# A one-core encoder step: first and last expert pair loaded in quarter matrices, last down weights by column blocks

## The reference, cut to what matters

```python
g_idx = argmax(x @ w_grp + b_grp)            # 4 groups
top_v, top_i = top_k(e_logits[g_idx], 2)     # 2 of the 4 experts in it
gate = one_hot(eid, 16) * g_w * softmax(top_v)
h = silu(einsum('nd,edf->nef', x, w1)) * einsum('nd,edf->nef', x, w3)
h = h * gate[..., None]
h_out = h_in + einsum('nef,efd->nd', h, w2)
y = rmsnorm(h_out) * g_final                 # y_prompt, y_sample
```

## Time and profile before

| | |
|---|---|
| median of 3 runs | 2102.23 us |
| the profiled execution: own time | 2103.92 us |
| its span, first to last instruction | 2102.1 us |
| busy: TensorE, VectorE, ScalarE, POOL | 96%, 29%, 12%, 3% |
| mean granted TensorE clock | 0.984 |
| chain that ended last: TensorE, DMA | 88%, 9% |
| DMA rate over the span; in the expert stage | 192 GB/s; 428 GB/s |

### The profile page before, as it was taken

How to read it: one execution, slowest core, us unless ns; L and a number is a source line. 1 busy time by engine, 2 the same in 40 slices (tenths; PEclk the granted TensorE clock), 3 DMA queues, 4 the chain that set the end, 5 groups by cost and what they waited for, 6 DMA issues and landing times.

```text
span 2102.1 us, 26593 instructions
## 1 busy us (share of the span) xinstructions
PE 2024.6 (96%) x11213; PEld 1359.1 (65%) x11213; DVE 606.6 (29%) x1622; ACT 255.3 (12%) x617; POOL 61.9 (3%) x116
## 2 busy tenths in 40 slices
PE   7999999999999999999999999999996999999996
PEld 4767788877777777777777777776773333333332
DVE  3053222212212443534535435321003222121212
ACT  2121112121201010110101101000011000000002
POOL 0010000000000000000000000000000000000000
PEclk9999999999999999999999999999997999999998
DMA  9563444433234132331332314266433999999996
GB/s 296 96 192 122 134 126 148 159 124 121 84 121 148 58 125 89 118 125 42 125 116 92 125 42 140 104 215 215 160 131 129 428 428 428 427 427 428 427 428 253
DMA packets 190666, 404.31 MB, mean 192 GB/s; under 512 B 11520, under 2 KB 165840, under 8 KB 176848
## 3 DMA queue, kind: packets, MB, share of 16 engines
q1 hardware_dynamic: 182064, 380.95, 49.7%
q0 software_dynamic: 6112, 18.61, 3.2%
q10 hardware_dynamic: 2368, 3.02, 0.4%
HBM read 391.87 MB, written 10.67 MB: 191 GB/s over the span
## 4 chain that ended last, share of the span: by engine, by line
PE 88%; DMA 9%; DVE 1%; DVEq 1%; issue 0%; ACT 0%; SPq 0%; ACTq 0%
PE bank L739 21%; PE bank L943 19%; PE bank L1155 7%; PE bank L945 6%; PE bank L1086 6%; PE bank L737 5%; PE bank L1188 3%; PE bank L1205 3%; PE bank L1053 3%; DMA ring<-in_w 3%; DMA Z<-in_w 3%; DMA SC<-in_w 3%; PE bank L988 1%; PE bank L994 1%; PE bank L716 1%; PE bank L852 1%
## 5 line engine op out<-in xcount | busy, mean ns | idle before, releaser
L739 PE MATMUL bank<-uT,ring 128*128 128x288 f32 (+2 forms) x1792 | 455.2, 411 | 0.6 <-DVE uT L1558 0.6
L943 PE MATMUL bank<-uT,ring 128*128 128x288 f32 x1536 | 406.4, 414 | 0.0
L739 PEld LDWEIGHTS bank<-uT,ring 128*128 128x128 f32 (+2 forms) x1792 | 334.2, 189 | 99.1 <-issue 8.2
L943 PEld LDWEIGHTS bank<-uT,ring 128*128 128x128 f32 x1536 | 283.1, 190 | 78.5 <-issue 3.1
L1155 PE MATMUL bank<-ring,Z 128*64 128x512 f32 x480 | 138.5, 611 | 7.0 <-issue 7.0
L945 PE MATMUL bank<-Z,ring 128*128 128x288 f32 x512 | 140.5, 418 | 0.0
L1086 PE MATMUL bank<-SC,ring 128*128 128x288 f32 x512 | 128.5, 410 | 1.1 <-DVEq L345 1.1
L1155 PE MATMUL bank<-Z 128*64 128x512 f32 x336 | 119.3, 615 | 5.1 <-issue 5.1
L737 PE MATMUL bank<-ring,Z 128*128 128x256 f32 x512 | 117.4, 383 | 0.0
L1086 PEld LDWEIGHTS bank<-SC,ring 128*128 128x128 f32 x512 | 96.1, 190 | 29.5 <-DVEq L345 1.6
L945 PEld LDWEIGHTS bank<-Z,ring 128*128 128x128 f32 x512 | 92.8, 190 | 25.5 <-issue 1.4
(11 more groups left out here) (385 smaller groups left out, 1796.2 us busy)
## 6 DMA issues: line engine op xcount, KB each, us to landing
ring<-in_w_in SPq DMA_DIRECT2D x102, 1024.0 KB, 7.9
ring<-in_w SPq DMA_DIRECT2D x42, 2048.0 KB, 31.5
Z<-in_w SPq DMA_DIRECT2D x33, 2048.0 KB, 30.5
SC<-in_w SPq DMA_DIRECT2D x21, 2048.0 KB, 29.4
ring<-in_w_mem_kv SPq DMA_DIRECT2D x16, 1024.0 KB, 6.8
ring<-in_w_o SPq DMA_DIRECT2D x16, 1024.0 KB, 7.6
ring<-in_p_b SPq DMA_DIRECT2D x8, 1024.0 KB, 5.3
ring<-in_p_m SPq DMA_DIRECT2D x8, 1024.0 KB, 8.0
```

Of the source, the lines that this page charges most:

```text
L739: ins = mm(bank[t][0:w, 0:T], rslot[q][:, c, w0:w0 + w], uT[:, c, :], start=c == 0, stop=c == KC - 1)
L943: ins = mm(b[:, 0:T], rslot[q][:, c, P * t:P * t + P], uT[:, c, :], start=c == 0, stop=c == last - 1)
```

## The change

1. In pair 0 and pair 7 a fill of w1 or w3 now holds a quarter of the rows of one matrix for both experts (the order is w1, w3 of quarter 0, w1, w3 of quarter 1 and so on). `up_fine` works in 8 steps of one fill each, and every step signals. A row piece that one DMA packet brings is 8 KB where it was 16 KB.
2. The last four fills (w2 of pair 7) hold 512 columns of both experts each, as two DMAs of 1 MiB in pieces of 2 KB. `last_down` finishes one bank with each of them and scatters the prompt tokens' block by block; the sample tokens come at the end.
3. The final norm's gain is multiplied into columns 0 to 1023 of `H` before the factor is known (`with_gain`), from two tiles that POOL loads early. ScalarE then scales these columns by the factor and sends them out from its own queue; VectorE does columns 1024 to 2047 in one piece for each tile, and `gains` loads half as much.
4. POOL's early loads grow from three to six, and TensorE and VectorE wait for all of them (`nk_in` 96).

```diff
+        K_COL = 12 * NPAIR - 4
+        def fine(i):
+            return i in (0, NPAIR - 1)
+        def hp_upto(i, fills):
+            return sum(8 if fine(x) else 4 for x in range(i)) + (fills if fine(i) else (fills + 1) // 2)
...
-        gB = ring[2][:, 0:D]
-        gB2 = ring[2][:, D:D + 512]
+        gB = (CON[:, K_M2:K_M2 + 512], Z_t[:, 15424:15936], ring[2][:, 0:1024])
+        gB2 = ring[2][:, 1024:1536]
...
+                if j_ < 8 and fine(i):
+                    q, w = divmod(j_, 2)
+                    return a[("w1", "w3")[w]][0][2 * i:2 * i + 2, 512 * q:512 * q + 512, :].rearrange("e (p c) n -> p e (c n)", c=4)
...
+                b = j_ - 8
+                return a["w2"][0][2 * i:2 * i + 2, :, 512 * b:512 * b + 512].rearrange("e (p c) n -> p e c n", c=4)
...
-                        sp.wait_ge(s("hp_mm"), 4 * i + j_ // 2 + 1)
+                        sp.wait_ge(s("hp_mm"), hp_upto(i, j_ + 1))
...
+                sp.wait_ge(s("hp_mm"), hp_upto(NPAIR - 1, 4))
                 gains()
...
+            for g in range(2):
+                pload(gB[g], dram_g[KC + 4 * g:KC + 4 * g + 4, :].rearrange("c p -> (c p)").partition_broadcast(P), "nk_in")
...
+                def up_fine(i):
+                    for st in range(8):
+                        q, w = divmod(st, 2)
+                        wv = arrived(12 * i + st).rearrange("p (x c n) -> p x c n", x=2, c=4)
+                        if w == 0:
+                            pe.wait_ge(s("xg_ev"), 4 * i + q + 1)
...
+                        for c in range(4):
+                            for x in range(2):
+                                ins = mm(bank[2 + w][sides[x], :], XG[:, 4 * q + c, sides[x]], wv[:, x, c, :],
+                                         start=q == 0 and c == 0, stop=q == 3 and c == 3)
+                        ins.then_inc(s("hp_mm"), 1)
+                        if st == 1 and i + 1 < NPAIR:
+                            pe.wait_ge(s("xg_ev"), 4 * i + 4)
+                            prepare(i + 1)
...
+                    columns(0)
+                    columns(1)
+                    pe.wait_ge(s("gp_ev"), i + 1)
+                    scatter(0)
+                    columns(2)
+                    scatter(1)
+                    columns(3)
+                    scatter(2)
+                    scatter(3)
+                    for g in range(4):
+                        ins = mm(bank[4][TS * g:TS * g + TS, :], GP[:, i % 2, TP:T], Yk[:, 512 * g:512 * g + 512], start=True, stop=True)
...
+            def left_half(tt):
+                act.wait_ge(s("rs_fin"), tt + 1)
+                A(H[:, tt, 0:1024], H[:, tt, 0:1024], ACT.Copy, scale=rsm[:, tt:tt + 1]).then_inc(s("y_left"), 1)
+                act.wait_ge(s("y_left"), tt + 1)
+                act.dma_start(o["y_p"][P * tt:P * tt + P, 0:1024], H[:, tt, 0:1024]).then_inc(s("out_y"), 16)
+            final_root(0)
+            token_squares(True, 8)
+            final_root(1)
+            left_half(0)
+            final_root(2)
+            left_half(1)
...
+                for g in range(4):
+                    for tt in range(2):
...
+                        V.tensor_tensor(h, h, bank[2 * (g % 2) + tt][:, :], ALU.add).then_inc(s("fin_add"), 1)
+                    if 1 <= g <= 2:
+                        with_gain(g - 1)
+                out_norm(0)
```

More of the change, by code:

```diff
@@ L582, in _ @@
             for t in range(2):
[L583 to L586, removed]
+                sp.wait_ge(s("y_done"), t + 1)
+                sp.dma_start(o["y_p"][P * t:P * t + P, 1024:2048], H[:, t, 1024:2048]).then_inc(s("out_y"), 16)
+            sp.wait_ge(s("y_done"), 3)
             for g in range(4):
@@ L1206, in down, with last_down, columns, scatter @@
                         ins.then_inc(s("sc_mm2"), 1)
+                def last_down(i):
+                    pe.wait_ge(s("hid_done"), i + 1)
+                    for f in range(4):
+                        ins = nc.tensor.transpose(bank[2][:, P * f:P * f + P], hid[:, f:f + 509:4], ident)
+                    ins.then_inc(s("ht_mm"), 1)
+                    pe.wait_ge(s("sc_add"), 9 * i)
+                    pe.wait_ge(s("ht_ev"), i + 1)
+                    def columns(b):
+                        wv = arrived(12 * i + 8 + b).rearrange("p (x c n) -> p x c n", x=2, c=4)
+                        for c in range(4):
+                            for x in range(2):
+                                ins = mm(bank[4 + b][sides[x], :], HS[:, c, sides[x]], wv[:, x, c, :], start=c == 0, stop=c == 3)
+                        ins.then_inc(s("yk_mm"), 1)
+                    def scatter(g):
+                        pe.wait_ge(s("yk_ev"), 4 * i + g + 1)
+                        for tt in range(2):
+                            t0, tn = TOK[tt]
+                            if g >= 2:
+                                pe.wait_ge(s("fin_add"), 2 * (g - 2) + tt + 1)
+                            mm(bank[2 * (g % 2) + tt][:, :], GP[:, i % 2, t0:t0 + tn], Yk[:, 512 * g:512 * g + 512],
+                               start=True, stop=True).then_inc(s("sc_mm2"), 1)
+                    columns(0)
[9 more added lines that the diff above has]
+                        ins = mm(bank[4][TS * g:TS * g + TS, :], GP[:, i % 2, TP:T], Yk[:, 512 * g:512 * g + 512], start=True, stop=True)
+                    ins.then_inc(s("sc_mm2"), 1)
                 prepare(0)
@@ L1212, in _ @@
                 gathered(0, range(4))
-                for i in range(EXPERTS // 2):
-                    up(i)
+                for i in range(NPAIR - 1):
+                    if fine(i):
+                        up_fine(i)
+                    else:
+                        up(i)
                     down(i)
+                up_fine(NPAIR - 1)
+                last_down(NPAIR - 1)
             with pe.Else():
@@ L2093, in _ @@
                         rows_in(i + 1)
-                    for n in range(9):
+                    for n in range(0 if last else 9):
                         tt, g = divmod(n, 4)
@@ L2144, in _ @@
                 dve.sem_inc(s("fin_add"), 9)
+                with_gain(0)
+                with_gain(1)
                 out_norm(0)
```

98 lines of the change are left out of this document (62 added, 36 removed).

## The result

The changed kernel takes 2095.78 us, the median of 8 runs (2095.35 to 2098.50), the kernel before 2102.48 in the same session (8 runs, 2101.79 to 2104.58): ratio 0.9968, 95% interval 0.9959 to 0.9976, or 6.7 us less. Forecast were 9.4 us less, 2092.8, and a range of 2089.8 to 2098.0. The profiled execution is the median one: its own time is 2095.78, its span 2094.0.

The account below looks back on a forecast made before the run. The expert-weight stream was taken to bound the kernel, with an open head and tail. Head -3.5, block 3's start +1.6 and tail -7.5 sum to -9.4 us: median 2102.23 becomes 2092.8, range 2089.8 to 2098.0.

Parts of the forecast that it names:

- What bounds the kernel: From some 1626 us the expert-weight stream bounds; a microsecond gained at its head or tail is one off the time.
- Head, -3.5: Pair 0's first step, 8 matmuls instead of 16, frees a buffer sooner: tenth fill issued 3.5 us earlier.
- The feared hole at the third fill: Rival: after pair 0's first step a late third fill leaves a hole up to 3.5 us: 2096.3; chance 0.10.
- The stream, +1.5: Last landing 1.5 us later from smaller pieces: +1.2 for four column fills at 403 GB/s, +0.3 for 8 KB pieces.
- packets cost more: Rival: column blocks run at the 1 KB rate, 354 GB/s; last landing moves by +4.4: 2095.6; chance 0.12.
- TensorE and DMA meet at block 3: In pair 7's end, block 3 lands at 2076.15 and TensorE starts it at 2076.4: a term of +1.6 us.
- Tail, -7.5: Work from block 3's start to the end takes 19.8 us instead of 27.3; bounds 18.5 to 22.
- 19.8: Tail's last step: VectorE's last product at 15.3 us plus 4.5 for stores, 2.36 MB being just inside.
- ScalarE's stores ending last: Sign at the kernel's end that, if seen, would show the prediction wrong.
- third rival: Last block lands late for another reason; only the head and norm's part (some 2 us) remain: 2098 to 2100; chance 0.04.
- Edits at nothing: POOL's three more loads, ScalarE's moved table load and the halved gains behind the last fill cost nothing.
- Slower by TensorE's clock: Rival: short waits at pair 7's end drop TensorE to 1.2 GHz; all at that level adds 23 us: 2115.8; chance 0.04.

Follow-up runs that it names:

- e1: Changed kernel with pair 0 back to half matrices of one expert and four steps: 2098.86 us, ratio 0.9986 to the kernel before.
- e5: Changed kernel without ScalarE's two stores of prompt columns 0 to 1023: 2094.19 us, ratio 0.9958 to the kernel before.
- e7: The changed kernel run once more, unaltered, as base for the other runs: 2095.50 us, ratio 0.9970 to the kernel before.
- e9: As e4, but pair 7's last four fills, down projection and scatters as before the change; quarter fills kept: 2101.41 us, ratio 0.9991 to the kernel before.
- e2: Changed kernel with only pair 7's up projection back to four steps over half matrices: 2098.88 us, ratio 0.9978 to the kernel before.
- e3: Changed kernel with the last four fills in 8 KB instead of 2 KB pieces, same bytes, output wrong: 2095.74 us.
- e11: Changed kernel with SP also issuing ScalarE's two stores of columns 0 to 1023: 2096.89 us, ratio 0.9969 to the kernel before.
- e4: Changed kernel with the final norm as before: VectorE alone, no early gain, SP stores all: 2094.71 us, ratio 0.9966 to the kernel before.
- e8: As e4, but the first tile's first norm piece is cut into two of 512 columns: 2096.03 us.
- e10: As e8, but each partition's w2 rows in the four column fills lie 128 apart, pieces still 2 KB: 2095.53 us.

## Why the prediction was right, and where it was off

*What bounds the kernel: right.* A microsecond at the head (e1) and at the tail (e5) came out at the end. The stream did not run dry: its DMA share is 1.01 to 1.05 in the stretches shown. Only the last three microseconds before the landing are not full, in the columns of the earlier trace rows:

```profile
2070.00:2073.00 3.00, 2.92 (x10) 0.80 (x6) 0.73 (x2) 0.72 (x2) 0.00 (x0) 1.00 0.75 238
```

Before the change the share fell only in the last 1.6 us (0.84 from 2073.0 to 2074.6). So some engines have run out while others still work on the last fill; what that costs is not separated here.

*Head, -3.5: right.* By the medians 3.1 to 3.6 (e1); by the profiles 7.40 - 3.62 = 3.8, or 7.76 - 4.53 = 3.2 from e1 and e7, which both began at the lower clock. The feared hole at the third fill did not come: each 2 us from 1624 to 1640 moved at 406 to 459 GB/s.

*The stream, +1.5: a term of the sum that was mis-sized.* It measured 3.0: the last landing is 449.0 us after the tenth fill's issue before (2074.65 - 1625.69) and 451.95 after. The four column fills, priced at p_a's 403 GB/s (+1.2), ran at 387: by that rate 21.7 us for 8.39 MB, +2.0. The 8 KB pieces, taken at +0.3, ran at 421: +0.6. e9 divides it nearly so: there, with 8 KB pieces but no column blocks, TensorE also waits for the last landing and starts at 450.0, 0.9 after the 449.1 of the kernel before, and the column blocks make the other 2.0. Both ends of the range held. The time measured, 2095.78, is also what the rival "packets cost more" gave (2095.6), but by chance: its 354 GB/s was not seen, and of the 2.7 us missed 1.3 lie in this term and 1.0 in the tail. The Trainium skill's page "DMA: Bandwidth & Descriptors" (section "Specifications") has line rate from 512 B on; the trace disagrees, with 387 at 2 KB, 421 at 8 KB and 427 at 16 KB. The prediction says that by this page the sum would be 1.5 us lower; by its own end of +0.5 for free packets, where TensorE alone bounds block 3, it is 1.1.

*TensorE and DMA meet at block 3: right.* TensorE waited 0.26 us for it; e2 and e3 show either side of the balance. It started 1.6 us earlier than the old products where 1.9 were forecast, but that this is so close is luck: in this profile pair 0 began 0.7 us earlier. Counted from the tenth fill's issue, block 3 came 2.9 us later where 1.6 were forecast, which is the term above.

*Tail, -7.5: off by one, in its last step.* The chain up to VectorE's last product was forecast to end 15.3 us after block 3 and ended at 14.6. The step that failed is "19.8": 4.5 us for the stores behind that product, with the 2.36 MB "also just inside". They were not: four pieces of 512 KB were issued from 2085.07 on within 2.2 us, the engines were full from 2086 to 2091 at 395 to 406 GB/s, and 6.2 us passed instead of 4.5. So this step was 1.7 us too low, and the 0.7 that the chain gave back hides part of it. The sign named for it, ScalarE's stores ending last, did not come: ScalarE issued its second at 2086.78, and the sample tokens' stores behind it, issued until 2091.25, end last. e5 and e11 show that the bytes set the end. The part on the norm, counted by me as a gain of some 2 us (third rival), is a loss of some 0.5 (e4).

*Profile to median.* The spans differ by 8.1 us, the medians by 6.7. The profiled execution before was 1.4 to 1.7 us above the median. Part of that lies before the experts: its first product at 1618.29 is later than in eight of the other twelve profiles of this study (1615.7 to 1618.9). Of the 8.1 us, 0.7 are this earlier start and 0.4 the head's 3.8 over the 3.4 taken below.

*Summed again with the measured terms:* -3.4 head, +3.0 landing (less 0.1 of wait), -6.5 tail = -7.0, against 6.7 and 7.2 less in the runs.

*Edits at nothing.* No run isolates POOL's three more loads. In e4, e8, e9 and e10, which have one more than before and not three, pair 0 begins at 1615.8 to 1618.9, in the changed kernel and its repeat at 1617.6 and 1616.3: no cost is seen, and it could be no larger than this spread.

*Slower by TensorE's clock: did not happen.* The granted clock is 1.00 in every window shown of the changed kernel up to the stores. TensorE's waits for DMA in the last pair's end were 0.39, 1.20 and 0.26 us. In e9, after a wait of 4.62 us, 32 counted matmuls took 8.84 us instead of 7.09 at a granted clock of 0.50 from 2062 to 2064: the mechanism is real, but no fall followed the shorter waits of the changed kernel. The Trainium skill's page "TensorE: Matmul & The Clock Gate" (section "HAM oscillation — how this bites in real kernels") has the clock fall again for each piece where the work on a piece is shorter than the DMA wait for the next. Here the waits are 1.20 us at most and the products of a block 3.65, so that condition is not met, and the trace agrees: the clock stays at 1.00. The prediction's "by it this rival would happen" read the page too widely.

## What to carry to other kernels

A stage bound by one stream of transfers has two open ends: the work that must finish before its first buffer is free, and the work after its last landing. Cut the first and the last transfers finer, and in the order in which results can be completed, but see that the engine is early enough for each piece, and price the smaller pieces from rows with the same size under a steady load. At the very end ask what the stores themselves need: a faster last computation hands them over in a bunch.

## What the runs showed of the hardware

- The weight stream with all DMA engines busy ran at 427 GB/s with 16 KB pieces, 420 to 421 with 8 KB and 387 with 2 KB, the last both with 8 KB and with 1 MiB between the pieces of a partition (e10); the short loads of p_a, 2 KB too, reached 403.
- SP's issue of a transfer can last long, the longer the smaller the pieces: eight column DMAs took it from 2023.61 to 2061.11, though the step that frees the last of their buffers ended at about 2037; with 8 KB pieces (e3) it was through at 2048.4. The engines stayed full in both. That SP waits for room in the queue is my reading of these times.
- ScalarE's table load (2056.92, behind its copy of `hid`) took 1.28 us and the next activation followed 0.01 us later, all inside its wait for block 0.
